# Seven experts' tokens moved by indirect DMA instead of one-hot matmuls

## The reference

```
logits = h @ w_router + b_router
top_val, top_idx = lax.top_k(logits, 2)
gates = softmax(top_val)
for each expert e, over the tokens routed to it:
    hb = silu(xb @ w1[e]) * (xb @ w3[e])
    out[tokens] += gate * (hb @ w2[e])
```

## Time and profile before

| | |
|---|---|
| time, three runs | 1684.65, 1685.31, 1686.38 us (median 1685.31) |
| span of the profiled execution | 1675.1 us; its own time is not recorded apart, the median of the runs is 10.2 us above the span |
| TensorE, VectorE, ScalarE, GpSimd busy | 1585.9, 1366.6, 1009.6, 33.2 us |
| mean granted TensorE clock | 0.980 of full |
| moved by DMA | 497 MB, of it 336 chunks of 1 MB of expert weights |

### The profile page before, as it was taken

The page is one execution under the profiler, slowest core; times in us unless marked ns, Lnnn a source line. Parts: engine busy times, 40 slices in busy tenths (PEclk is TensorE's granted clock), DMA queues, the critical chain, the costliest instruction groups (busy, mean ns, idle before and its releaser), DMA issues.

```text
span 1675.1 us, 21955 instructions
## 1 busy us (share of the span) xinstructions
PE 1585.9 (95%) x8462; PEld 1361.2 (81%) x8462; DVE 1366.6 (82%) x1239; ACT 1009.6 (60%) x868; POOL 33.2 (2%) x77
## 2 busy tenths in 40 slices
PE   3979989999898997999999999999999999999995
PEld 3869979999778996888788788788788788788784
DVE  7986587775886658898898898898898898898885
ACT  3554444343454444777677677677677677777673
POOL 5000000000000000000000000000000000000000
PEclk9999999999997998999999999999999999999998
DMA  9856568765672752999999999999999999999991
GB/s 375 322 194 237 201 232 298 279 253 184 206 291 96 255 181 77 378 357 344 357 354 347 356 354 344 358 354 346 361 351 346 356 352 351 359 352 350 343 370 49
DMA packets 69874, 497.00 MB, mean 297 GB/s; under 512 B 7824, under 2 KB 7952, under 8 KB 11024
## 3 DMA queue, kind: packets, MB, share of 16 engines
q1 hardware_dynamic: 68528, 491.40, 78.9%
q0 software_dynamic: 1248, 4.20, 0.9%
HBM read 494.52 MB, written 1.05 MB: 296 GB/s over the span
## 4 chain that ended last, share of the span: by engine, by line
PE 88%; DVE 7%; ACT 3%; DMA 1%; issue 1%; SPq 0%; DVEq 0%; ACTq 0%
PE ps L1233 27%; PE ps L1235 26%; PE ps L1234 26%; PE ps L1597 2%; PE ps L1505 1%; PE ps L1576 1%; DMA x_tok<-in_x_dram 1%; DVE lo L767 1%; DVE ada_acc L731 1%; PE ps L1385 1%; DVE r L819 1%; PE ps L1272 1%; ACT r L563 1%; PE ps L1252 1%; DVE x_tok L854 1%
## 5 line engine op out<-in xcount | busy, mean ns | idle before, releaser
L798 DVE TENSOR_TENSOR lo<-raw,hi 128x2048 fp32r<-128x2048 f32 x336 | 766.0, 2290 | 116.8 <-ACT hi L462 116.2
L462 ACT ACTIVATE hi<-raw 128x2048 fp32r<-128x2048 f32 x336 | 645.1, 1920 | 228.2 <-PE ps L1235 228.1
L1233 PE MATMUL ps<-hi,hT_hi 128*128 128x512 f32 (+2 forms) x1088 | 431.7, 397 | 9.9 <-DVE hT_lo L825 4.4
L1235 PE MATMUL ps<-hi,hT_lo 128*128 128x512 f32 (+2 forms) x1088 | 420.5, 386 | 0.0
L1234 PE MATMUL ps<-lo,hT_hi 128*128 128x512 f32 (+2 forms) x1088 | 419.7, 386 | 0.0
L767 DVE TENSOR_TENSOR lo<-raw,hi 128x2048 fp32r<-128x2048 f32 (+2 forms) x87 | 189.2, 2181 | 87.1 <-ACT hi L446 85.9
L1233 PEld LDWEIGHTS ps<-hi,hT_hi 128*128 128x128 f32 x1088 | 205.2, 189 | 53.9 <-issue 9.9
L446 ACT ACTIVATE hi<-raw 128x2048 fp32r<-128x2048 f32 (+2 forms) x87 | 158.2, 1824 | 136.7 <-PE ps L1235 132.6
L1233 PE MATMUL ps<-hi,bT_hi 128*128 128x512 f32 (+1 forms) x576 | 232.9, 404 | 8.1 <-DVE lo L767 6.2
L1234 PEld LDWEIGHTS ps<-lo,hT_hi 128*128 128x128 f32 x1088 | 205.3, 189 | 41.1 <-issue 3.4
L1235 PEld LDWEIGHTS ps<-hi,hT_lo 128*128 128x128 f32 x1088 | 204.9, 188 | 41.1
(11 more groups left out here) (238 smaller groups left out, 1286.4 us busy)
## 6 DMA issues: line engine op xcount, KB each, us to landing
raw<-in_moe_w_dram SPq DMA_DIRECT2D x336, 1024.0 KB, 6.8
raw<-in_w_ada_dram SPq DMA_DIRECT2D x48, 1024.0 KB, 6.3
raw<-in_w_fg_dram SPq DMA_DIRECT2D x11, 1024.0 KB, 5.8
raw<-in_w_fu_dram SPq DMA_DIRECT2D x11, 1024.0 KB, 5.1
raw<-in_w_fd_dram SPq DMA_DIRECT2D x11, 1024.0 KB, 5.7
raw<-in_w_ga_dram SPq DMA_DIRECT2D x8, 1024.0 KB, 7.0
raw<-in_w_gb_dram SPq DMA_DIRECT2D x8, 1024.0 KB, 5.5
raw<-in_w_ab_dram SPq DMA_DIRECT2D x8, 1024.0 KB, 6.8
```

The source lines that it names most:

```text
L462: act.activation(hi[:, s, :], raw[:, slot, :], ACT.Copy).then_inc(hi_done, 1)
L798: dve.tensor_tensor(lo[:, s, :], raw[:, slot, :], hi[:, s, :].bitcast(f32), ALU.subtract).then_inc(raw_done, 1)
L1233: pe.matmul(o, wh, mh, start=first, stop=False)
L1235: return pe.matmul(o, wl, mh, start=False, stop=last)
```

## The change

Expert 0 is still gathered by matmuls, and expert 7 (and spare items) still scattered by matmuls. Between them the tokens go through DRAM:

- Two internal DRAM tensors are added: `rows_x` (256 x 1024) with the tokens times 1/rms, and `rows_y` (384 x 1024), zeroed in its first 256 rows; its last 128 rows take what empty slots write.
- In the first item VectorE also writes a plain one-hot of expert 0 and the normed tokens `xn`; GpSimd stores `xn` to `rows_x`.
- `select(i+1)` moves from group 4 to group 2. In group 3 TensorE multiplies the one-hot by three columns of values, token number, one and gate (`slot_rows`), and VectorE makes the row numbers from it (`rows`): the gather row, and a scatter row that points to the spare rows where the slot is empty.
- GpSimd gathers 128 rows of 4 KB into `x_rows` by indirect DMA. In groups 5 and 6 TensorE only transposes them (`turn_rows`).
- ScalarE multiplies the result by the gate while it copies it (`weighted_y`), and GpSimd adds the 128 rows to `rows_y` by an indirect DMA with addition. After the seventh, `rows_y` is read back into `y_exp`, where the drain adds expert 7.
- The gate transposes, their copy, the four scatters and the four additions remain for expert 7 only.

```diff
+            pool.dma_start(rows_y[0:SEQ].rearrange("(t p) d -> p t d", p=P), y_exp).then_inc(rows_out, 16)
+            pool.wait_ge(xn_ready, 1)
+            pool.dma_start(rows_x.rearrange("(t p) d -> p t d", p=P), xn).then_inc(xn_out, 16)
+            pool.wait_ge(xn_out, 16)
+            for i in range(EXPERTS):
+                if i + 1 < EXPERTS:
+                    pool.wait_ge(idx_ready, i + 2)
+                    pool.indirect_dma_start(out=x_rows[:, :], out_offset=None, in_=rows_x,
+                                            in_offset=bass.IndirectOffsetOnAxis(ap=gidx[:, 0:1], axis=0)).then_inc(rows_in, 16)
+                    pool.wait_ge(rows_out, 16 * (i + 1))
+                    pool.wait_ge(m_yc, i + 1)
+                    pool.indirect_dma_start(out=rows_y, out_offset=bass.IndirectOffsetOnAxis(ap=sidx[:, i % 2:i % 2 + 1], axis=0),
+                                            in_=r5[:, :], in_offset=None, compute_op=ALU.add).then_inc(rows_out, 16)
+            pool.wait_ge(rows_out, 16 * EXPERTS)
+            pool.dma_start(y_exp, rows_y[0:SEQ].rearrange("(t p) d -> p t d", p=P)).then_inc(y_in, 16)
...
+            def weighted_y(i, par, last):
+                act.wait_ge(used, i * PER_ITEM + (NW + last + 1))
+                act.wait_ge(rows_out, (i + 1) * 16)
+                act.activation(r5[:, :].rearrange("p (c s) -> p c s", c=2), ps[:, 4:6, :], ACT.Identity,
+                               scale=held[:, par, 2:3]).then_inc(m_yc, 1)
...
+            def rows(i, par, later=True):
+                dve.wait_ge(idx_full, i + 1)
+                if later:
+                    dve.wait_ge(rows_out, i * 16)
+                dve.tensor_copy(gidx[:, :], ps[:, 7, 0:1])
+                dve.tensor_copy(held[:, par, :], ps[:, 7, 0:4]).then_inc(v_rows, 1)
+                dve.wait_ge(v_rows, 2 * i + 1)
+                dve.scalar_tensor_tensor(srow[:, :], held[:, par, 1:2], ndump[:, :], held[:, par, 0:1], ALU.mult, ALU.add).then_inc(v_rows, 1)
+                dve.wait_ge(v_rows, 2 * i + 2)
+                dve.tensor_scalar(sidx[:, par:par + 1], srow[:, :], dump[:, :], None, ALU.add).then_inc(idx_ready, 1)
...
                     if ahead:
+                        for t in range(T):
+                            m = one_hot(t, 1.0)
+                        m.then_inc(first_hot, 1)
+                        for t in range(T):
+                            m = dve.tensor_scalar(xn[:, t, :], x[:, t, :], rstd[:, T + t:T + t + 1], None, ALU.mult)
+                        m.then_inc(xn_ready, 1)
                         spares()
...
-                    if ahead and g == 4:
-                        dve.wait_ge(m_gt, i + 1)
-                        select(i + 1)
+                    if ahead and g == 2:
+                        select(i + 1, True)
...
+                    if first and ahead and g == 1:
+                        rows(i, par, False)
+                    if ahead and g == 3:
+                        rows(i + 1, 1 - par)
...
+            def slot_rows():
+                for t in range(T):
+                    m = pe.matmul(ps[:, 7, 0:4], r4[:, t * P:(t + 1) * P], vals[:, t, :], start=(t == 0), stop=(t == T - 1))
+                m.then_inc(idx_full, 1)
+
+            def turn_rows(part):
+                for kk in range(4):
+                    k = 4 * part + kk
+                    m = pe.transpose(ps[:, 7, kk * P:(kk + 1) * P], x_rows[:, k * P:(k + 1) * P], ident[:, :])
+                m.then_inc(m_gath, 1)
...
                     if g == 1 and not first:
                         pe.wait_ge(m_yc, i)
-                        scatter(i - 1, 0)
+                    if ahead and g == 3:
+                        pe.wait_ge(m_pos, i + 2)
+                        pe.wait_ge(idx_ready, i + 1)
+                        slot_rows()
                     if ahead and g == NG - 2:
-                        pe.wait_ge(m_gtc, i + 1)
-                        pe.wait_ge(m_pos, i + 2)
-                        gather(i + 1, 0)
+                        pe.wait_ge(rows_in, i * 16 + 16)
+                        turn_rows(0)
                     if ahead and g == NG - 1:
                         pe.wait_ge(m_xf, i * 2 + 3)
-                        gather(i + 1, 1)
+                        turn_rows(1)
```

More of the change, by code:

```diff
@@ L53 @@
 LAG_SUM, LAG_USE = 3, 6
+SETUP = 10 + SPARE + HALF
 f32 = mybir.dt.float32
@@ L216, in build @@
         pos_tab, gate_tab = (sb(n, [P, T, ITEMS]) for n in ("pos_tab", "gate_tab"))
-        pg = sb("pg", [P, 2, T])
+        pg = sb("pg", [P, T])
+        vals = sb("slot_vals", [P, T, 4])
+        held = sb("slot_held", [P, 2, 4])
+        dump, ndump = sb("dump_row", [P, 1]), sb("neg_dump_row", [P, 1])
+        gidx, sidx = sb("gather_row", [P, 1], i32), sb("scatter_row", [P, 2], i32)
+        srow = sb("scatter_row_f", [P, 1])
+        rows_x = nc.dram_tensor("rows_x", [SEQ, D], f32, kind="Internal").ap()
+        rows_y = nc.dram_tensor("rows_y", [SEQ + P, D], f32, kind="Internal").ap()
         info = sb("info", [P, ITEMS + 1], i32)
@@ L238, in build @@
         y_exp = r6[:, 0:T * D].rearrange("p (t d) -> p t d", t=T)
+        xn = r6[:, T * D:2 * T * D].rearrange("p (t d) -> p t d", t=T)
+        x_rows = acc
         ws = r7[:, :].rearrange("p (g t) -> p g t", g=GROUPS)
@@ L285, in build @@
         m_yc, m_sc, m_acc = sem("m_yc"), sem("m_sc"), sem("m_acc")
+        xn_ready, xn_out, y_zero = sem("xn_ready"), sem("xn_out"), sem("y_zero")
+        first_hot, idx_full, idx_ready = sem("first_hot"), sem("idx_full"), sem("idx_ready")
+        rows_in, rows_out, y_in = sem("rows_in"), sem("rows_out"), sem("y_in")
         out_done = sem("out_done")
-        v_step, v_loop = sem("v_step"), sem("v_loop")
+        v_step, v_loop, v_rows = sem("v_step"), sem("v_loop"), sem("v_rows")
         p_step = sem("p_step")
@@ L369, in _ @@
             pool.iota(eidx_i, pattern=[[1, EXPERTS]], base=0, channel_multiplier=0).then_inc(p_step, 1)
-            pool.wait_ge(p_step, 8 + SPARE + HALF)
+            pool.iota(tok_i, pattern=[[P, T]], base=0, channel_multiplier=1).then_inc(p_step, 1)
+            pool.memset(vals[:, :, :], 1.0).then_inc(p_step, 1)
+            pool.wait_ge(p_step, SETUP)
             pool.affine_select(out=ident[:, :], in_=ident[:, :], compare_op=ALU.not_equal, fill=1.0, base=0,
@@ L388, in link @@
                 pool.wait_ge(p_step, steps[0])
[L390 removed]
+            steps = [SETUP]
             TWO_PI = 2.0 * np.pi
@@ L397, in _ @@
             LIMIT = float(np.nextafter(np.float32(np.pi), np.float32(0)))
+            pool.tensor_copy(vals[:, :, 0], tok_i)
+            pool.tensor_scalar(dump[:, :], tok_i[:, 0:1], float(SEQ), None, ALU.add)
+            pool.tensor_scalar(ndump[:, :], tok_i[:, 0:1], -1.0, -float(SEQ), ALU.mult, ALU.add)
             pool.wait_ge(small_in, 32)
@@ L669, in item @@
                         hidden_hi(i - 1, NG - 1)
-                    if g == 3:
-                        act.wait_ge(m_gt, i + 1)
+                    if g == 3 and not ahead:
+                        act.wait_ge(m_gt, i - (EXPERTS - 2))
                         act.activation(r4[:, 512:512 + SEQ], ps[:, 7, 0:SEQ], ACT.Copy).then_inc(m_gtc, 1)
@@ L679, in drain @@
                 hidden_hi(i, NG - 1)
+                if isinstance(i, int):
+                    act.wait_ge(rows_out, 16 * (i + 1))
                 copy_y(i, PER_ITEM - 1)
@@ L1097, in one_hot, with select @@
             def one_hot(t, value):
-                return dve.tensor_scalar(r4[:, t * P:(t + 1) * P], slots[:, :], pg[:, 0, t:t + 1], value, ALU.is_equal, ALU.mult)
+                return dve.tensor_scalar(r4[:, t * P:(t + 1) * P], slots[:, :], pg[:, t:t + 1], value, ALU.is_equal, ALU.mult)
             def gate_hot(t):
-                return dve.tensor_scalar(r4[:, 256 + t * P:256 + (t + 1) * P], slots[:, :], pg[:, 0, t:t + 1], pg[:, 1, t:t + 1],
+                return dve.tensor_scalar(r4[:, 256 + t * P:256 + (t + 1) * P], slots[:, :], pg[:, t:t + 1], vals[:, t, 2:3],
                                          ALU.is_equal, ALU.mult)
-            def select(i):
-                dve.tensor_copy(pg[:, 0, :], pos_tab[:, :, bass.ds(i, 1)].rearrange("p t o -> p (t o)"))
-                dve.tensor_copy(pg[:, 1, :], gate_tab[:, :, bass.ds(i, 1)].rearrange("p t o -> p (t o)")).then_inc(v_loop, 1)
+            def select(i, by_row):
+                dve.tensor_copy(pg[:, :], pos_tab[:, :, bass.ds(i, 1)].rearrange("p t o -> p (t o)"))
+                dve.tensor_copy(vals[:, :, 2], gate_tab[:, :, bass.ds(i, 1)].rearrange("p t o -> p (t o)")).then_inc(v_loop, 1)
                 dve.wait_ge(v_loop, i + 1)
                 for t in range(T):
-                    one_hot(t, rstd[:, T + t:T + t + 1])
+                    one_hot(t, 1.0 if by_row else rstd[:, T + t:T + t + 1])
                     m = gate_hot(t)
@@ L1120, in select_first @@
                 gates()
```

(48 more changed lines are left out.)

14 lines of the change are left out of this document (8 added, 6 removed).

## The result

The changed kernel takes 1646.55 us (median of 4 runs, 1643.81 to 1650.43) against 1684.98 (4 runs, 1682.41 to 1686.38): ratio 0.9774, 95% interval 0.9753 to 0.9795, so 38.4 us less between the medians. The forecast was 1648, from -37.2 us. The profiled execution of the changed kernel took 1650.43 us, with a span of 1648.7; the other three spanned 1642.1, 1642.9 and 1646.7.

A forecast was written before the change was run, and what follows sets the result against it. TensorE's instruction stream was taken to bound the expert stage. -44.5 removed + 3.8 added + 1.4 stalls + 2.1 first expert = -37.2 us, from median 1685.31 to 1648; bounds 1642 to 1664, stated range 1642 to 1667.

The forecast's parts named there:

- TensorE sets the pace and what leaves it leaves the time: Expert stage: TensorE's stream alone sets the 125.00 us period per expert, which falls to about 119.3 us.
- What is removed: TensorE: 28 scatters 24.1 us, 14 gather halves turned into transposes 18.9, seven experts' gate transposes 1.5; sum 44.5 us.
- 0.1 of stall: Groups 5 and 6: with shorter gather cover TensorE waits about 0.1 us for VectorE's low part, 14 times, 1.4 us.
- What is added: TensorE: two small fp32 matmuls eight times, 0.48 us a time from the router's 128x8 row, 3.8 us in all.
- The stall of 0.28 behind the selection: Selection moved from group 4 to 2 keeps its 0.28 us stall; removing it would gain 1.7 us, the lower bound.
- First expert: Two one-hots and two scalings on VectorE ahead of the routing table add 2.1 us, bounds 1.4 and 3.1.
- ScalarE's scaled copy: Copy of y, about 1 us, becomes an Identity with per-partition scale; taken at nothing.
- The DMAs: Gather has 24.4 us to land, scatter 45 us, stream needs 378 to 382 GB/s; all taken as hidden, nothing added.
- Rival 2: Loads cannot exceed about 352 GB/s for long, so an item takes 128.1 us: 1709 us, slower; chance 0.05.
- Rival 1: DMA engines become the bound mildly, ceiling 371 GB/s from rate over busy share: 1664 to 1673 us; chance 0.12.
- Rival 4: Feed stalls from VectorE's and ScalarE's order or an adding DMA, 1 to 3 us an item: 1655 to 1669; chance 0.10.
- The frame around the sum: Median 1685.31 exceeds the profiled 1675.1 us span by 10.2, left unchanged: 1638 span, 1648 time.

The follow-up runs named there:

- experiment 1: Changed kernel with four fp32 512-column matmuls put back on TensorE in each item after the first, their result unused: 1670.88 us.
- kernels 5 and 7: Changed kernel with 5: first expert's one-hots and scalings after routing table, `gathered_lo` behind next low part, 1642.03 us; 7: also TensorE's, VectorE's and ScalarE's loops written out, 1643.05 us.
- experiments 2 and 3: Changed kernel with two, then five further 1 MB loads per item from the POOL queue, read by nothing: 1648.63 us, then 1661.46 us.
- kernels 2, 3, 4, 6 and 8: Changed kernel with 4: slot rows made in group 4, not 3, 1673.31 us; 6: TensorE's loop written out, 1648.07 us; 8: nothing altered, 1647.06 us; 2, 3 above.

## Why the prediction was right

*TensorE sets the pace and what leaves it leaves the time.* Right. Forecast 119.3 us a period, measured 119.36 where no loop turns back; experiment 1 gives back what it puts in.

*What is removed.* The scatters brought 3.56 an item instead of 3.44. Each gather half was to bring 1.35 less 0.1 of stall; it brought 1.15. The transposes cost the 0.44 that was said; the stall is 0.16 to 0.19, not 0.1, 14 times: +1 us against the sum. The prediction placed it correctly (the chunk behind the turn, late by VectorE) and kernels 5 and 7 take it away by the cause that it named.

*What is added.* `slot_rows` 0.34 and 0.11 for the slower matmul behind it, 0.45 against 0.48. The router's 128x8 row was the right neighbour.

*The stall of 0.28 behind the selection* was misread. The piece of 0.28 in the earlier trace rows stands where 0.23 is normal, so it held 0.05 and not 0.28; the group with the selection took 16.90 against 16.78 elsewhere. With the selection moved, both groups take 16.81 in the period shown. It was "carried along" in the sum and so cost nothing, but the lower bound built on it, 1.7, had at most 0.7 in it.

*First expert.* The start grew by 1.66 us, forecast 2.1, inside 1.4 to 3.1. The mechanism is the one described; kernels 5 and 7 show it by removing it.

*ScalarE's scaled copy.* The Identity with a scale takes 1.09 us (L686 above), the plain copy that is left in the drain (L680) 1.03. Nothing of it is on the path.

*The DMAs.* Gather 10.6 us of a window of 24.4, scatter 11.4 of 45, rate 373 to 383 against the 378 to 382 forecast. Rival 2 doesn't hold here: one core alone drew 373, 395 and 415 GB/s over 840 us and more. The prediction read the Trainium skill ("DMA: Bandwidth & Descriptors", Bandwidth) too narrowly: the same section gives about 358 GB/s to each core when both cores of a memory domain stream, and measured 425 for one core with its neighbour idle. This case bears out the second figure, with 415 at most. Rival 1's arithmetic, rate divided by busy share, fell with experiments 2 and 3. Rival 4 came in its mildest form, as the 0.16 to 0.19 above.

*What the sum left out.* The loop-back. The two groups in which the loop turns took 0.78 and 0.70 us longer than the same group without it before, 1.23 and 2.54 after: +2.3 us. In the second profile of the changed kernel they took 1.06 and 1.23 longer, +0.8 us. The first profile also lost 1.7 us in the drain, where behind the last expert the matmuls ran at half pace for 3.4 us (0.43 for 0.23; granted clock 0.53 from 1622.9 us on; 21.11 us for 19.42 from the last turn to ScalarE's copy). That is no part of the change: the second profile has 1.00 there and takes 19.50. Without these terms the first profiled pair would read -37.2 and the second -37.0, against the sum's -37.2. So close an agreement is in part luck, since the sum's own parts were off by up to 1.3 us in either direction: the gather +1.3, the scatters -0.8, the start -0.4.

*The frame around the sum was wrong, without harm.* "10.2 more for what lies around the span" is not what lies around it: in every run of the changed kernel time and span differ by 1.7 to 1.8 us, and in a run of before too (1671.08 and 1669.3). The span of 1675.1 was that of an execution that happened to be fast ahead of the experts. Adding the difference was right only because it turned that execution into the typical one; the forecast of the span, 1638, was accordingly below all four measured (1642.1 to 1648.7). The 38.4 us between the medians are therefore not more exact than the 33.2 and 36.2 of the traces. Executions of like mean clock, 0.973 or 0.974, spanned 1684.2 to 1686.2 us in the kernel before and 1648.7 and 1649.4 in the changed one, some 36 us apart.

## What to carry over

Where one engine is busy 99% of a stage, sum up what leaves and enters that engine's stream, from rows of the same form, and check the others only for whether they keep up: it came out to 0.1 us in 119, in part because errors cancelled, and it missed the loop-backs, which aren't instructions of the stream. Judge a DMA ceiling by a stretch in which the loads ran faster, not by today's rate or busy share. When the profiled execution lies far from the median of the runs, look for its clock in the stretches that the change doesn't touch before the difference is booked to anything; and profile the changed kernel twice before a loss of 1 or 2 us is booked to the change.

## What the hardware showed that was not expected

The stretch ahead of the experts has two forms. Granted clock from 100 to 200 us, and start of the matmuls that build the routing table: 1.00 and 649.0 to 650.6 us in the profiled executions of before and of kernels 1, 5 and 7; 0.90 to 0.91 and 655.9 to 658.5 us in those of after and of kernels 2, 3, 4, 6 and 8. The kernels with changes behind it fall on both sides, so the change doesn't decide it; some 7 us of the spread of the times, the whole size of experiments 5 to 8, is this. What decides it was not found.

A TensorE that ends a pass of its loop stands 1.0 to 2.0 us with nothing that the profile shows to wait for, or waits 2.1 to 2.5 for a low part; before the change it stood 0.4 to 0.5 (1024.80 and 1275.60 us in its chain), and it doesn't when the loop is written out. Why the change made it longer was not tried. The POOL engine is held for 2.7 us to issue a gather of 128 rows of 4 KB and for 2.0 us for an adding scatter, against 0.54 for a plain load; both land within 12.6 us beside a stream of 373 GB/s, about what the plain load took at worst.
